# Seven products also in the MLP's way down, for the six middle chunks, with streamed way-up operands

## What is computed

```python
def squared_relu_mlp(h, w_up, w_down):
    return jnp.square(jax.nn.relu(h @ w_up)) @ w_down
...
        x = x + squared_relu_mlp(rms_norm(x, mlp_norm[l]), w_up[l], w_down[l])
```

## Time and profile before

| | us |
|---|---|
| runs: median of 3 | 3433.12 |
| runs: lowest, highest | 3431.18, 3434.05 |
| profiled execution: its span | 3430.4 |
| one chunk of the MLP (16 in all) | 81.7 |
| of it way up (168 matmuls), way down (192) | 38.08, 43.67 |

### The profile page before, as it was taken

The page is one execution under the profiler, slowest core; times in us unless marked ns, Lnnn a source line. Parts: engine busy times, 40 slices in busy tenths (PEclk is TensorE's granted clock), DMA queues, the critical chain, the costliest instruction groups (busy, mean ns, idle before and its releaser), DMA issues.

```text
span 3430.4 us, 43111 instructions
## 1 busy us (share of the span) xinstructions
PE 3379.4 (99%) x16026; PEld 2788.4 (81%) x16026; DVE 1962.6 (57%) x2418; ACT 1205.7 (35%) x2072; POOL 1260.6 (37%) x828
## 2 busy tenths in 40 slices
PE   8999999999999999999999999999999999999999
PEld 7778888888888887777888888887888888778887
DVE  6666662844454477884384444457746546545445
ACT  6446651422222245764142222224524233102011
POOL 1121214444445440024344445453435345323340
PEclk9999999999999999999999999999999999999999
DMA  5010012111111121111211111113111111111241
GB/s 214 21 42 18 24 58 86 49 50 50 50 49 50 54 108 60 46 46 65 78 49 50 50 49 50 60 58 107 37 59 58 43 61 45 64 46 62 93 148 66
DMA packets 67634, 211.84 MB, mean 62 GB/s; under 512 B 7280, under 2 KB 11888, under 8 KB 65680
## 3 DMA queue, kind: packets, MB, share of 16 engines
q1 hardware_dynamic: 56848, 165.04, 14.6%
q10 hardware_dynamic: 10624, 44.63, 3.6%
HBM read 186.32 MB, written 22.02 MB: 61 GB/s over the span
## 4 chain that ended last, share of the span: by engine, by line
PE 92%; DVE 5%; issue 1%; POOL 1%; ACT 1%; DMA 1%; ACTq 0%; DVEq 0%; SPq 0%; POOLq 0%
PE G L885 37%; PE G L1303 20%; PE AUX L1253 17%; PE G L1545 3%; PE G L1124 2%; PE AUX L1186 2%; PE AUX L1424 2%; PE AUX L1322 2%; PE AUX L1176 1%; PE G L1007 1%; PE AUX L1166 1%; PE AUX L1053 1%; PE AUX L1303 1%; PE AUX L1506 1%; DVE probs L2553 1%
## 5 line engine op out<-in xcount | busy, mean ns | idle before, releaser
L885 PE MATMUL G<-Hhi,whi 128*128 128x512 f32 x1552 | 631.6, 407 | 7.3 <-DVE Hlo L2682 2.8
L885 PE MATMUL G<-Hhi,wlo 128*128 128x512 f32 x1552 | 605.9, 390 | 0.0
L885 PE MATMUL G<-Hlo,whi 128*128 128x512 f32 x1552 | 605.4, 390 | 0.0
L685 POOL CAST whi<-wraw 128x1024 fp32r<-128x1024 f32 (+1 forms) x123 | 135.6, 1102 | 1101.4 <-PE G L885 592.7
L1303 PE MATMUL G<-u_hi,slot_hi 128*128 128x512 f32 x992 | 387.7, 391 | 0.0
L1303 PE MATMUL G<-u_lo,slot_hi 128*128 128x512 f32 x992 | 386.2, 389 | 0.0
L1303 PE MATMUL G<-u_hi,slot_lo 128*128 128x512 f32 x992 | 386.1, 389 | 0.0
L885 PEld LDWEIGHTS G<-Hhi,whi 128*128 128x128 f32 x1552 | 292.1, 188 | 74.4 <-issue 7.1
L734 POOL TENSOR_TENSOR slot_lo<-raw_down,slot_hi 128x512 fp32r<-128x512 f32 x144 | 190.2, 1321 | 416.4 <-ACT slot_hi L1923 416.2
L885 PEld LDWEIGHTS G<-Hlo,whi 128*128 128x128 f32 x1552 | 292.3, 188 | 62.5 <-issue 5.7
L885 PEld LDWEIGHTS G<-Hhi,wlo 128*128 128x128 f32 x1552 | 291.7, 188 | 61.8
(11 more groups left out here) (463 smaller groups left out, 6890.8 us busy)
## 6 DMA issues: line engine op xcount, KB each, us to landing
wraw<-wjobs SPq DMA_DIRECT2D x148, 512.0 KB, 3.4
raw_down<-down_pairs SPq DMA_DIRECT2D x64, 512.0 KB, 3.4
raw_up<-up_units SPq DMA_DIRECT2D x30, 512.0 KB, 3.7
raw_up<-up_units SPq DMA_DIRECT2D x44, 256.0 KB, 3.3
mw_raw<-wjobs SPq DMA_DIRECT2D x16, 512.0 KB, 5.2
scratch<-X ACTq DMA_DIRECT2D x2, 4096.0 KB, 13.0
gate_tiles<-gate_st ACTq DMA_DIRECT2D x16, 512.0 KB, 4.1
T<-gate_tiles ACTq DMA_DIRECT2D x16, 512.0 KB, 3.5
```

The source lines that it names most:

```text
L685: pool.tensor_copy(whi[:, par, 0:kt], wraw[:, par, 0:kt]).then_inc(w_hi, 1)
L885: mm = pe.matmul(G[:, par if psum is None else psum, cols], w[:, par, k, :], x[:, k, cols], start=(i == 0 and j == 0), stop=(i == kt - 1 a ...
```

## The change

Chunks 0 and 7 (`WHOLE`) keep their way down. In chunks 1 to 6 the way down is also done with seven products, twice (g = 0 and 1, for two halves of the output features): `unit_down`, 7 x 2 x 2 x 3 = 84 matmuls each. A chunk is then 28 products of 12 matmuls in a row.

- For that, the blocks of u need their own sums t1 to t4 and the high and low parts of all seven operands. They are formed in SBUF tiles `d_sum`, `d_hi`, `d_lo`, of 512 columns, for both halves h. VectorE makes the squares, sums and lows (`unit_up`), ScalarE the casts (`high_of_u`).
- Room for these tiles comes from t4, which loses its place: t4 and b21 share one place and are read back by SP from HBM in turn, 2 MB each time, four DMAs (`load_shared`). In chunk 0 both are stored to HBM once a layer.
- Weights come as whole units of 1 MB (`load_unit`), into two buffers by turns. GpSimd works through each unit in `unit_weights`. In the way down the sums s1 and s3 are made by VectorE (`weight_sums`), s2 and s4 by GpSimd.
- A product of the way down is added into X as soon as it is done (`add_product`, 1024 columns), 14 times a chunk, with no factor r2. In chunk 0 X is instead multiplied by the factor's inverse ahead of the add, and in chunk 7 all of X is multiplied by r2. The reciprocal moves behind chunk 0's adds.
- The products of the way up have a new order (`UP_ORDER`), and chunk 7 of the way up uses the same code.

The core of the diff, cut:

```diff
+WHOLE = (0, CHUNKS - 1)
+MIDDLE = CHUNKS - len(WHOLE)
+CHUNK_USES = [2 * PRODUCTS + (KT if c in WHOLE else 2 * PRODUCTS) for c in range(CHUNKS)]
...
+FACTORS = {"p1": ("a11", "b11"), "p2": ("a12", "b21"), "p3": ("s4", "b22"), "p4": ("a22", "t4"),
+           "p5": ("s1", "t1"), "p6": ("s2", "t2"), "p7": ("s3", "t3")}
+UP_ORDER = (("p1", "p4", "p6", "p5", "p7", "p3", "p2"), ("p1", "p2", "p6", "p5", "p7", "p3", "p4"))
+DOWN_ORDER = ("p1", "p5", "p6", "p3", "p7", "p2", "p4")
+CHAINED = ("p1", "p6", "p7", "p4")
...
+LOW_ORDER = (("t3", "b11", "t1", "b22", "b21", "t2", "t4"), ("b11", "t1", "t2", "b22", "t3", "b21", "t4"))
...
+            def load_unit(l, c, h):
+
+                src = up_units[(l * CHUNKS + c) * 2 + h] if h < 2 else down_units[(l * MIDDLE + c - 1) * 2 + h - 2]
+                sp.dma_start(raw_unit[h % 2][:], src).then_inc(up_in[h % 2], 16)
+
+            def load_shared(n):
+
+                for half in range(2):
+                    ks = slice(2 * half, 2 * half + 2)
+                    for part in range(2):
+                        sp.dma_start(b21[part][:, ks, :].bitcast(F32), operand_tiles[n, part][:, ks, :]).then_inc(shared_in[half], 16)
...
+                for c in range(1, CHUNKS):
+                    for h in range(2):
+
+                        sp.wait_ge(m_used, use_of(l, c, h, 1) + 1)
+                        load_shared(1 - h)
+                        if c not in WHOLE:
+                            sp.wait_ge(m_lo, use_of(l, c, h, PRODUCTS - 1) + 1)
+                            load_unit(l, c, 2 + h)
+                        elif h == 0:
...
-                for i in range(1, 4):
-                    load_down(l, CHUNKS - 1, i)
+                        for h in range(2):
+                            sp.wait_ge(m_lo, use_of(l, c, 2 + h, PRODUCTS - 1) + 1)
...
+            def unit_weights(l, c, h):
+
+                a11, a12, a21, a22 = (raw_unit[h % 2][:, i, :] for i in range(4))
+                pool.wait_ge(up_in[h % 2], raw_of(l, c, h) * 16)
+                pool.wait_ge(m_lo, use_of(l, c, h, 0))
+                if h < 2:
+                    pool.tensor_tensor(s1_sum[:], a21, a22, ALU.add).then_inc(m_sum, 1)
+                    pool.tensor_tensor(a21, a11, a21, ALU.subtract).then_inc(m_sum, 1)
+                for j, name in enumerate(products_of(c, h)):
+                    n = use_of(l, c, h, j)
+                    low(n, raw_block(h, FACTORS[name][0]))
+                    if name == "p1":
+                        pool.wait_ge(m_lo, n + 1)
+                        pool.wait_ge(m_sum, unit_of(l, c, h) * 4 + 2)
+                        pool.tensor_tensor(a11, s1_sum[:], a11, ALU.subtract).then_inc(m_sum, 1)
+                    elif name == "p6":
+                        pool.wait_ge(m_lo, n + 1)
+                        pool.tensor_tensor(a11, a11, a12, ALU.subtract).then_inc(m_sum, 1)
...
+                def unit_up(c, h):
+
+                    a, copied, read = 3 * h, copied_to(l, c, h), read_to(l, c, h)
+                    if c > 1 and h == 0:
+                        pe.wait_ge(m_exit, read - 7 + 2)
+                    elif c > 1:
+                        pe.wait_ge(h_sums, f_sum(l, c - 1, 1, "b21"))
...
+                    else:
+                        pe.wait_ge(m_exit, read)
+                        factor(c, h, 1, 2, True)
+                        pe.wait_ge(m_x, copied + 1)
+                        factor(c, h, 2, a, False)
+                        factor(c, h, 3, 1, True)
+                        pe.wait_ge(m_x, copied + 2)
+                        factor(c, h, 4, a, False)
+                        pe.wait_ge(m_x, copied + 3)
+                        factor(c, h, 5, 1, False)
+                        pe.wait_ge(m_exit, read + 2)
+                        factor(c, h, 6, a, False)
...
+                def unit_down(c, g):
+
+                    for j, name in enumerate(DOWN_ORDER):
+                        n, op = use_of(l, c, 2 + g, j), FACTORS[name][1]
+                        par, start = g if name in CHAINED else 1 - g, name in ("p1", "p5", "p2")
+                        if name in ("p6", "p7", "p4"):
+                            pe.wait_ge(m_out, added(l, c, g, {"p6": "p1", "p7": "p6", "p4": "p7"}[name]))
+                        elif name in ("p3", "p2"):
+                            pe.wait_ge(m_out, added(l, c, g, {"p3": "p5", "p2": "p3"}[name]))
...
+                        pe.wait_ge(m_lo, n + 1)
+                        for h in range(2):
+                            if g == 0:
+                                pe.wait_ge(m_ul, f_low(l, c, h, op))
+                            for i in range(2):
+                                w = slice((2 * i + h) * P, (2 * i + h + 1) * P)
+                                for s, (a, x) in enumerate(((slot_hi, d_hi), (slot_hi, d_lo), (slot_lo, d_hi))):
+                                    mm = pe.matmul(G[:, par, i * HALF:(i + 1) * HALF], a[slot_of(n)][:, w], x[h][op][:],
+                                                   start=(start and h == 0 and s == 0), stop=(h == 1 and s == 2),
+                                                   skip_group_check=not start)
+                        mm.then_inc(m_used, 1)
...
+                def unit_up(c, h):
+
...
+                    for j, name in enumerate(UP_ORDER[h]):
+                        n = use_of(l, c, h, j)
+                        if name in copies:
+                            block, bank = copies[name]
+                            act.wait_ge(m_used, n + 1)
+                            if whole and h:
+                                act.wait_ge(m_ul, tiles_to(l, c, 1))
+                            act.copy(block_of_u(c, h, block), AUX[:, bank, :]).then_inc(m_x, 1)
+                        ahead(n)
+                        if h == 0:
+                            if j == 5:
+                                high_of_u(c, 0, "b22", "b21")
+                            elif j == 6:
+                                high_of_u(c, 0, *(("b12", "b11") if whole else ("t3",)))
+                        elif j == 0 and not whole:
+                            high_of_u(c, 0, "b11", "t1", "t2", "t4")
+                        elif j == 2:
+                            high_of_u(c, 1, "b11")
+                        elif j == 5:
+                            high_of_u(c, 1, "b22")
+                        elif j == 6:
+                            high_of_u(c, 1, *(("b12", "b21") if whole else ("t1", "t2", "t3")))
...
             def add_down(l, c, m):
-                dve.wait_ge(m_used, use_of(l, c, 2, m) + 1)
+
                 bank = down_bank(c, m)
-                chain.link(dve.tensor_tensor(bank, bank, r2[:], ALU.mult))
-                dve.tensor_tensor(X[:, m, :], bank, X[:, m, :], ALU.add).then_inc(m_out, 1)
+                if c == 0:
+                    chain.link(dve.tensor_tensor(X[:, m, :], X[:, m, :], r2[:], ALU.mult))
+                    dve.wait_ge(m_used, use_of(l, c, 2, m) + 1)
+                    dve.tensor_tensor(X[:, m, :], bank, X[:, m, :], ALU.add).then_inc(m_out, 1)
+                else:
+                    dve.wait_ge(m_used, use_of(l, c, 2, m) + 1)
+                    chain.link(dve.tensor_tensor(X[:, m, :], bank, X[:, m, :], ALU.add))
+                    dve.tensor_tensor(X[:, m, :], X[:, m, :], r2[:], ALU.mult).then_inc(m_out, 1)
...
+                    if h == 0:
+                        after(4, 4)
+                        dve.tensor_tensor(b22_, a, b22_, ALU.subtract).then_inc(m_exit, 1)
+                        dve.tensor_tensor(b21_, a, b21_, ALU.add).then_inc(m_exit, 1)
+                        square("b22", 1)
+                        square("b21", 2)
+                        after(5, 4)
+                        dve.tensor_tensor(b12_, b12_, d, ALU.subtract).then_inc(m_exit, 1)
+                        square("b12", 3)
+                        total("t3", "b22", "b12", ALU.subtract, "b12")
+                        after(6, 4)
+                        dve.tensor_tensor(b11_, e, b11_, ALU.add).then_inc(m_exit, 1)
+                        square("b11", 4)
+                        total("t1", "b11", "b12", ALU.subtract, "b11")
+                        total("t2", "b22", "t1", ALU.add, "t1")
+                        total("t4", "b21", "t2", ALU.subtract, "t2")
+                        if whole:
+                            finish()
+                        else:
+                            dve.wait_ge(h_sums, f_sum(l, c, h, "t4"))
+                            low_of_u(*LOW_ORDER[0])
+                        return
+                    after(1, 1)
+                    dve.tensor_tensor(b11_, e, b11_, ALU.add).then_inc(m_exit, 1)
+                    square("b11", 1)
+                    after(4, 3)
+                    dve.tensor_tensor(b22_, a, b22_, ALU.subtract).then_inc(m_exit, 1)
+                    square("b22", 2)
+                    if not whole:
+                        weight_sums(c, 0)
+                    after(5, 3)
```

(71 more changed lines are left out.)

383 lines of the change are left out of this document (268 added, 115 removed).

## The result

The changed kernel takes 3514.3 us (median; 3512.9 to 3515.2), the kernel before 3432.7 in the same comparison: ratio 1.0239, 95% interval 1.0224 to 1.0253. It is slower by 2.4%; forecast was 3509.

A forecast was written before the change was run, and what follows sets the result against it. TensorE bounds the kernel; the change makes VectorE late through the SBUF port shared with GpSimd. Span 3430.4 + 12 x 5.8 (middle chunks) + 6 (chunk 7) = 3506, plus 2.7 to the runs' median: 3509 us; range 3412 to 3548.

The forecast's parts named there:

- Bound and gain: TensorE bounds the MLP chunks; fewer way-down matmuls save 5.59 us a chunk, 67 us in 12 chunks, until another engine is late.
- VectorE's window: Middle chunk, walked op by op: 30 VectorE operations before product 14's low of b11 overrun 25.6 us; 23 have two SBUF inputs.
- the faster rival: Two-input VectorE operations average under 1.14 us, so the kernel gets faster: 3420 us (0.17) or 3366 (0.03), in all 0.20.
- (a): Middle chunk, product 8: b11's exit and GpSimd's low come late; 0.4 to 1.1 us late, 0.4 taken.
- (b): Middle chunk, product 11: ScalarE casts sums ahead of the product's weights, after VectorE alternates with GpSimd; 0.6 us late.
- (c): Middle chunk, product 12: half 0's lows delay b11's square, and ScalarE's copy of product 10's bank waits behind it; 3.2 us late.
- (d): Middle chunk, second half of product 14: b11's low comes behind weight sums and operations alternating with GpSimd; 5.2 us late.
- (e): Middle chunk, product 16: the add of p1 into X stands behind VectorE's remaining sums and lows; 2.0 us late.
- The clock: Half-speed matmuls after TensorE's gaps were priced at 0, being hidden by other lateness; full price 5 us a chunk.
- Chunk 7: Later lows before the first down tile (2 us) and r2's multiply with two SBUF inputs (1): +3 us a layer, 6 total.
- GpSimd's sums: Two way-down weight sums per half moved to VectorE, counted in (d); leaving them on GpSimd would add 4 x 1.29 us there.
- The pair's price: One two-SBUF-input VectorE operation and one GpSimd operation together cost 1.70 us; at 1.97, total 3557 us (0.01).

The follow-up runs named there:

- e9_last_order_no_gpsimd: `e8_psum_last_order` with GpSimd's weight sums and low parts of chunks 1 to 6 left out, so the output is not the reference's; 3374.5 us, ratio 0.9829.
- e3_sums_back: The changed kernel with the two weight sums of each way-up half moved back from VectorE to GpSimd; 3524.6 us, ratio 1.0263.
- e11_two_waits_less: `e8_psum_last_order` with p7's addition ahead of t4's low in chunks 1 to 6, and chunk 7's b11 copy waiting for one low; 3378.6 us, ratio 0.9847.
- e8_psum_last_order: `e4_blocks_in_psum` with VectorE's list reordered, finally p3's addition ahead of b21's low and chunk 7's b11 exit ahead of two lows; 3385.5 us, ratio 0.9858.
- e4_blocks_in_psum: The changed kernel with squares of b11, b22, b21 and sum t3 of each half written to free PSUM banks, not SBUF; 3436.8 us, ratio 1.0012.

## Why the prediction was right, point by point

- *Bound and gain.* Right: the matmuls are worth 5.59 us a chunk. With GpSimd silent and the last order (`e9_last_order_no_gpsimd`) a chunk is 76.3 us, 5.5 under the 81.75 before, so the stream from HBM and ScalarE's time are no bound, as costed. TensorE had no wait for a DMA at product 6.
- *VectorE's window.* Right. Forecast from 13.8 to 48.8 us into the chunk; in the chunk from 786.64 it runs from 13.8 (800.45) to 48.6 (835.24). The 23 two-input instructions average 1.28 us (29.35 us summed over the timeline) against 1.26 in the walk and the deciding 1.14 of the faster rival.
- *(a)* 0.4 forecast, 0.6 measured. *(b)* 0.6 at product 11 did not come: in the case in which product 8 waits longer, product 11 waits less, as the walk said.
- *(c)* 3.2 forecast, 2.83 measured, by the chain named: lows end at 34.25 (34.3), copy at 36.7 (36.8).
- *(d)* 5.2 forecast, 3.17 idle. The end was right to 0.2 us; what was wrong is when TensorE asked. Its 30 matmuls from 823.41 to 832.12 took 8.7 us and not 6.8, at half clock. So 1.9 of the 5.2 shows as slow work and not as waiting: the prediction's paragraph on the clock said that these slow products lie beside (d), and the total did not change.
- *(e)* 2.0 forecast, 0.35 on average measured (4.2 in 12 chunks). Where the clock stayed up behind (d), in two chunks, the add was late by 1.76 and 1.77, near the forecast. In the other ten the slow products took its place, as the clock's paragraph said, and the wait is 0.29 or less. Sum forecast 11.4 a chunk, measured 11.3; 87.6 against 87.53.
- *The clock.* Adding 0 was right, because the slow products lie where VectorE or an add would have been late anyway: product 14's second half started 48.65 us into the chunk (48.6 in all twelve), 9.25 late, against a forecast of 9.4 for (a) to (d), and what comes behind it is 2.05 on average against the 2.0 of (e). The two chunks with the full clock behind (d) take 87.55 us each, the ten others 87.52 on average. So that fall of the clock cost nothing on average; but single chunks with it take 86.8 to 88.3 us, and that slow work and a late add come to the same mean is in part luck. Behind (c) from 5 to 9 matmuls ran slow, and product 14's second half started at the same 48.6 us; no run took that fall away altogether, so its price by itself is not shown.
- *Chunk 7* was mis-sized: +3 a layer forecast, +5.75 measured. The term looked at the lows ahead of the first down tile (1.1 us) and at the multiplication by r2. It missed ScalarE's copy of half 1's b11 into T, which in the changed code waits for all four lows of half 0 (2.6 us), and the half-clock products behind it (about 2 us). This is the 5 us by which the time came out above 3509.
- *GpSimd's sums.* The walk had them delay (d): done at 41.75 us, b12's exit behind them. They were done at 41.55, but the exit starts no earlier without them (`e3_sums_back`: 41.4), since product 12, at half clock, ends later than in the walk. So in that place they cost next to nothing. Leaving them on GpSimd costs 10 us more, and not in the place where the prediction looked.
- *The pair's price.* 1.70 us a pair carried the sum; 1.97 would have given 3557, which is 43 us too much. The changed kernel shows 1.70 again, where t1 and t2 of half 0 alternate with GpSimd, whose operations end at 811.37 and 813.07:

```profile
809.75 1.62 POOL L937 TENSOR_TENSOR raw_odd<-raw_odd 128x512 f32<-128x512 f32 x1
811.34 1.73 POOL L881 TENSOR_TENSOR slot_lo<-s_sum,slot_hi 128x512 fp32r<-128x512 f32 x1
```

- *The rivals* fell for the reason given: the faster one needed a mean under 1.14, which was reached only with GpSimd's work left out or the inputs moved.

## What to carry to other kernels

Before moving work of TensorE to VectorE, count the instructions with two SBUF inputs that run beside GpSimd and price them at the pair (here 1.70 us), not at their own 0.68; then walk the list against the time at which TensorE asks. If it does not fit, first take an input of these instructions to PSUM (here 78 us), and order the list only then (58 us more, to `e11_two_waits_less`; without PSUM nearly the order of `e8_psum_last_order` gave 10).

## What was not expected of the hardware

- The granted clock read 0.50 behind gaps of 2.83 us (above), 3.17, and 2.3, but not behind every such gap: it stayed at 1.00 behind 3.18 us (747.74, above). In `e4_blocks_in_psum` TensorE waited 1.76 and 1.77 us ahead of two products (821.36 and 827.52), and the stretches behind them read 1.00:

```profile
821.00:824.00 3.00, 2.64 (x11) 2.17 (x12) 2.96 (x4) 1.57 (x3) 2.12 (x3) 1.00 0.00 0
...
827.00:830.00 3.00, 2.48 (x11) 2.06 (x12) 3.00 (x5) 0.26 (x1) 1.29 (x1) 1.00 0.00 0
```

- Work moved from VectorE to GpSimd can cost VectorE more than it takes off it: moving two sums a down half to GpSimd, which in the changed kernel is busy for 56 of a chunk's 87 us, made the kernel 10 us slower (`e3_sums_back`). The chunk's row in the table of stretches (GpSimd's is the fifth busy time):

```profile
786.82:873.80 86.98, 80.37 (x337) 64.98 (x337) 59.45 (x56) 28.60 (x49) 56.11 (x41) 0.96 0.28 97
```

The prediction had 65 us for it, too much by 9: fewer than 33 of its operations met one of VectorE's.
